# The mixers of a layer in two phases instead of four

## The reference, cut to what matters

```python
h = rmsnorm_2(x, norm1_g) * (1.0 + sc1) + sh1
a, mq, mk, mv, mo, mg, dq, dk, dv = jnp.split(h @ w_in, splits, axis=-1)
conv_l = conv_module(a, ...)      # u = a1 * sigmoid(a2); 31 taps; layernorm over channels; silu
mlstm_l = mlstm_mixer(...)        # 4 heads of 64, forwards and backwards, gates scanned over time
diff_l = diff_mixer(...)          # 4 heads: rotary; p = softmax(q1 k1) - lam * softmax(q2 k2); p @ v; rmsnorm
mix = jnp.concatenate([conv_l, mlstm_l, diff_l], axis=-1)
x = x + g1 * (mix @ w_out)
...
x = x + g2 * peer_ffn(h2, ...)
```

## Time and profile before

| | |
|---|---|
| median of 3 runs | 4462.64 us (4460.4 to 4464.87) |
| the profiled execution's own time | 4458.87 us |
| its span | 4457.1 us |
| TensorE busy | 4037.1 us, 91% |
| DVE, ScalarE, GpSimd busy | 53%, 37%, 34% |
| mean granted TensorE clock | 0.935 |
| layer 0: input blocks / stages 2 to 4 | 945.0 to 1090.7 / to 1336.3 us |
| layer 1: input blocks / stages 2 to 4 | 3224.0 to 3348.5 / to 3511.2 us |

### The profile page before, as it was taken

One profiled execution on the slowest core, in us unless ns is written; L12 is line 12 of the kernel. 1 busy time (PEld: TensorE's weight loads), 2 busy tenths in 40 slices (PEclk: granted clock), 3 DMA queues, 4 the chain that ended last, 5 costly groups with the idle time before them and its releaser, 6 DMA issues. The chain is left out here.

```text
span 4457.1 us, 71091 instructions
## 1 busy us (share of the span) xinstructions
PE 4037.1 (91%) x25218; PEld 3528.5 (79%) x25218; DVE 2383.2 (53%) x4156; ACT 1640.7 (37%) x2529; POOL 1527.5 (34%) x605
## 2 busy tenths in 40 slices
PE   7997698978858999999989999999796699999998
PEld 7974388956525999988879999888684499998887
DVE  4012413144651946687538466885535375667855
ACT  3532204132122443333545433334432245333344
POOL 5840007223002886500028866000060088660000
PEclk9997899989569999999999999999895799999999
DMA  5565545522002554444645544446430155444454
GB/s 185 180 221 178 179 151 152 162 73 80 3 0 90 167 164 138 135 146 146 193 148 164 166 140 136 142 143 190 136 109 12 44 166 174 139 139 141 145 180 151
DMA packets 168398, 613.86 MB, mean 138 GB/s; under 512 B 18592, under 2 KB 20000, under 8 KB 167968
## 3 DMA queue, kind: packets, MB, share of 16 engines
q1 hardware_dynamic: 168224, 611.49, 43.9%
HBM read 610.37 MB, written 1.05 MB: 137 GB/s over the span
## 5 line engine op out<-in xcount | busy, mean ns | idle before, releaser
L1644 POOL TENSOR_TENSOR ring_r<-ring,ring_hi 128x1024 fp32r<-128x1024 f32 x408 | 1065.2, 2618 | 1260.8 <-ACT ring_hi L1781 1259.7
L1781 ACT ACTIVATE ring_hi<-ring 128x1024 fp32r<-128x1024 f32 x792 | 837.8, 1059 | 788.6 <-DMA ring<-in_peer_v 478.4
L1659 PE MATMUL bank<-H_r,ring_hi 128*128 128x256 f32 x3264 | 938.4, 288 | 63.3 <-POOL ring_r L1644 60.3
L1660 PE MATMUL bank<-H_r,ring_hi 128*128 128x256 f32 x3264 | 926.0, 284 | 0.0
L1661 PE MATMUL bank<-H_r,ring_r 128*128 128x256 f32 x3264 | 925.5, 284 | 0.0
L1659 PEld LDWEIGHTS bank<-H_r,ring_hi 128*128 128x128 f32 x3264 | 628.3, 192 | 71.3 <-POOL ring_r L1644 44.9
L277 POOL TENSOR_TENSOR ring_r<-ring,ring_hi 128x1024 fp32r<-128x1024 f32 x183 | 455.3, 2493 | 603.1 <-ACT ring_hi L271 602.6
L1660 PEld LDWEIGHTS bank<-H_r,ring_hi 128*128 128x128 f32 x3264 | 628.6, 193 | 0.0
L1661 PEld LDWEIGHTS bank<-H_r,ring_r 128*128 128x128 f32 x3264 | 628.3, 192 | 0.0
L1711 PE MATMUL bank<-ring_hi,H_r 128*128 128x512 f32 x1536 | 483.8, 396 | 4.5 <-DVE ring_r L1955 4.4
L1713 PE MATMUL bank<-ring_r,H_r 128*128 128x512 f32 x1536 | 474.6, 390 | 0.0
(11 more groups left out here) (312 smaller groups left out, 5469.1 us busy)
## 6 DMA issues: line engine op xcount, KB each, us to landing
ring<-in_peer_u SPq DMA_DIRECT2D x384, 512.0 KB, 3.5
ring<-in_peer_v SPq DMA_DIRECT2D x384, 512.0 KB, 3.5
ring<-in_w_in SPq DMA_DIRECT2D x135, 512.0 KB, 3.5
ring<-in_ada SPq DMA_DIRECT2D x96, 512.0 KB, 5.3
ring<-in_w_f SPq DMA_DIRECT2D x72, 512.0 KB, 3.6
ring<-in_w_br SPq DMA_DIRECT2D x24, 512.0 KB, 3.6
ring<-in_w_q SPq DMA_DIRECT2D x24, 512.0 KB, 3.5
ring<-in_w_out SPq DMA_DIRECT2D x16, 512.0 KB, 3.5
```

The lines of the kernel that those rows point to most:

```text
L1644: pool.tensor_tensor(ring_lo[:, slot, :], ring[:, slot, :], ring_hi[:, m % NH, :].bitcast(F32), ALU.subtract).then_inc(p_lo, 1)
L1659: pe.matmul(o, hi[:, k], x_hi_[:, kt, :], start=(kt == 0), stop=False)
L1660: pe.matmul(o, hi[:, k], x_lo_[:, kt, :], start=False, stop=False)
L1781: act.activation(ring_hi[:, m % NH, :], ring[:, (n0 + m) % NS, :], ACT.Copy).then_inc(a_hi, 1)
```

## The change

Stages 2 to 4 become two things. The scans, the value and state transposes, the rotation and the convolution's norm move into the phase of the input blocks, each behind a certain block; there TensorE now uses banks 0 to 3 for the blocks and waits for the evacuation four before, banks 4 to 7 serve the moved work. The blocks of `w_in` come in another order (gates, convolution, recurrence values, attention values, queries, keys, recurrence keys, queries, output gates). One phase remains: a loop over four heads with four steps each, and an item of the attention in each step (every second step in the last layer). The weights are no longer scaled and subtracted on DVE: DVE writes two diagonal matrices with the factors, and TensorE multiplies each of the two exponentials by its diagonal, which scales, subtracts and transposes at once. The diagonal pieces of the recurrence are masked by a maximum with 10000 in the exponent instead of a product. The convolution's root and the heads' roots come before the reciprocal, with the scale folded in. The large work tile of the recurrence lies where `h_high` was, other tiles in `H`.

```diff
@@ phase of the input blocks @@
+                    pool.memset(Bt, 0.0)
+                    pool.memset(Mx, 0.0)
+                    pool.memset(on, 1.0).then_inc(padded, 1)
+                    for b in range(2):
+                        low(pool, n0, b, a_hi, p_lo)
                     pool.memset(u_pad, 0.0).then_inc(padded, 1)
+                    pool.memset(v_aug, 1.0).then_inc(padded, 1)
...
+                    def turn_values(n, src, b):
+                        pe.wait_ge(by_act, evac[:b + 1].count("act"))
+                        if n:
+                            pe.wait_ge(a_vt, n)
+                        for tt in range(4):
+                            mm = pe.transpose(bank[7][:, tt * P:(tt + 1) * P], src[:, tt * P:(tt + 1) * P], ident)
+                        mm.then_inc(vt_ps, 1)
...
-                        evac_wait(pe, {"act": by_act, "dve": by_dve}, evac, b, 6)
+                        evac_wait(pe, {"act": by_act, "dve": by_dve}, evac, b, 4)
...
+                        if b == 6:
+                            turn_state()
+                        if b in (8, 9):
+                            turn_values(b - 8, mv[:, b - 8, :], b - 3)
+                        if 10 <= b < 14:
+                            turn_values(b - 8, dv[:, b - 10, :], b - 3)
...
+                        if b == 19:
+                            pe.wait_ge(v_tap, 2 * CONV_K)
...
+                        if b >= 17:
+                            rotate(b - 17)
...
                         if b + NH < 25:
                             high(act, n0, b + NH, a_hi)
+                        if b == 0:
+                            act.wait_ge(by_dve, 1)
+                            link(act.activation(Lt, fg, ACT.Abs))
+                            link(act.activation(Lt, Lt, ACT.Exp, scale=-1.0))
+                            act.activation(Lt, Lt, ACT.Ln, bias=1.0).then_inc(a_soft, 1)
...
+                        if 9 <= b < 15:
+                            keep_values(b - 9)
...
@@ the one phase behind it, TensorE @@
+                    def turn_weights(n):
+                        pe.wait_ge(v_p, n + 1)
+                        if n:
+                            pe.wait_ge(a_pt, n)
+                        for k in range(keys_of(n) // P):
+                            o, c = bank[6][:, k * P:(k + 1) * P], slice(k * P, (k + 1) * P)
+                            pe.matmul(o, E[:, n % 2, 0, c], diag[:, n % 2, 0, :], start=True, stop=False)
+                            mm = pe.matmul(o, E[:, n % 2, 1, c], diag[:, n % 2, 1, :], start=False, stop=True)
+                        mm.then_inc(pt_ps, 1)
...
+                        for k in range(4):
+                            if k == 0:
+                                broadcast(h, 0)
+                                products(h, 0)
+                                products(h, 1)
+                                if h:
+                                    values(h - 1, 1)
+                            if k == 1:
+                                broadcast(h, 1)
+                            if k == 2:
+                                products(h, 2)
+                                products(h, 3)
+                            if k == 3:
+                                values(h, 0)
+                            n = item_of(h, k)
+                            if n is not None:
+                                if n + 1 < N:
+                                    scores(n + 1)
+                                if n:
+                                    attend(n - 1)
+                                turn_weights(n)
...
@@ ScalarE @@
+                            if k == 1:
+                                decays(h, 0)
+                            if k == 2:
+                                decays(h, 1)
+                            n = item_of(h, k)
+                            if n is not None:
+                                if n + 1 < N:
+                                    softmax(n + 1)
+                                keep_weights(n)
+                                if n % per_head == 0 and n:
+                                    squares(n // per_head - 1, n)
+                                if n % per_head == 1 and n > per_head:
+                                    root(n // per_head - 1)
...
@@ VectorE @@
+                            if k == 0:
+                                if h:
+                                    finish(h - 1, 0)
+                                exponents(h, 0)
+                            if k == 1:
+                                if h:
+                                    finish(h - 1, 1)
+                                exponents(h, 1)
+                            if k == 2:
+                                weigh(h, 0)
+                                weigh(h, 1)
+                            if k == 3:
+                                weigh(h, 2)
+                                weigh(h, 3)
+                            n = item_of(h, k)
+                            if n is not None:
+                                shares(n)
+                                if n + 1 < N:
+                                    maxima(n + 1)
+                                if n:
+                                    keep(n - 1)
```

More of the change, by code:

```diff
@@ L1244, in build, with item_of @@
             ms = A.take(16)
+            dg = A.take(1)
             tiles = list(range(t0 // P, 4))
+            tall = len(tiles)
+            per_head = 2 if last else 4
+            items = [(h, qt) for h in range(DF_H) for qt in (range(2, 4) if last else range(4))]
+            N = len(items)
+            keys_of = lambda n: T if items[n][1] < 2 else 2 * T
+            def item_of(h, k):
+                if last:
+                    return 2 * h + k // 2 if k % 2 else None
+                return 4 * h + k
@@ new lines, in values @@
+                    def values(h, d):
+                        pe.wait_ge(v_w, 8 * h + 8)
+                        if h or d:
+                            pe.wait_ge(v_h, 2 * h + d)
+                        for tt in tiles:
+                            src = sources(d, tt)
+                            for st in src:
+                                mm = pe.matmul(bank[3][:, tt * 65:tt * 65 + 65], wb[:, d, st, tt * P:(tt + 1) * P],
+                                               v_aug[:, st, h, :], start=(st == src[0]), stop=(st == src[-1]))
+                        mm.then_inc(pv_ps, 1)
@@ new lines, in scores @@
+                    def scores(n):
+                        h, qt = items[n]
+                        for s in range(2):
+                            if n:
+                                pe.wait_ge(a_exp, 2 * (n - 1) + s + 1)
+                            r = slice(64 * s, 64 * s + 64)
+                            pe.matmul(bank[4 + s][:, 0:keys_of(n)], dq[r, h, qt * P:(qt + 1) * P], dk[r, h, 0:keys_of(n)],
+                                      start=True, stop=True).then_inc(ds_ps, 1)
+                    def turn_weights(n):
[7 more added lines that the diff above has]
+                        mm.then_inc(pt_ps, 1)
@@ new lines, in attend @@
+                    def attend(n):
+                        h = items[n][0]
+                        pe.wait_ge(a_pt, n + 1)
+                        if n:
+                            pe.wait_ge(v_o, n)
+                        done = max(0, (n - 1) // per_head)
+                        if n % per_head == 1 and done:
+                            pe.wait_ge(a_root, done)
+                        nk = keys_of(n) // P
+                        for k in range(nk):
+                            mm = pe.matmul(bank[7][:, 0:P], dv_tok[:, k, h * P:(h + 1) * P], pT[:, n % 2, k * P:(k + 1) * P],
+                                           start=(k == 0), stop=(k == nk - 1))
+                        mm.then_inc(o_ps, 1)
@@ L1419, in _ @@
+                    finish(ML_H - 1, 0)
+                    keep(N - 1)
+                    finish(ML_H - 1, 1)
+                    if per_head == 2:
+                        normed(DF_H - 2)
+                    a = tiles[0]
                     hv = hs[:, a:4, :, :].rearrange("p t h e -> p (t h) e")
```

599 lines of the change are left out of this document (269 added, 330 removed).

## The result

The changed kernel takes 4391.1 us (median of 4, 4387.19 to 4394.96) where the kernel before took 4461.52 in the same job (4 runs): ratio 0.9844, 95% interval 0.9827 to 0.9861, some 70 us less. The forecast was 51 us less. Its profiled execution took 4394.96 us, span 4392.9.

A forecast was written before the change was run, and what follows sets the result against it. TensorE, 91% busy, was taken as the bound, with 408.3 us of slow-clock mixer stretches to win from. Gains of 41 us (layer 0) and 10 (layer 1) from 4458.9 gave 4408, 4411 on the median's scale; 8-in-10 range 4365 to 4465.

The forecast's parts named there:

- The sum of layer 0: Layer 0's mixer: blocks 26, before the loop 4, loop 155, tail 19.5, together 204.5 against 245.6 us, gain 41 us.
- Blocks, +26 us each: Input blocks of both layers: moved work and TensorE's waits for ScalarE's copies lengthen each layer's blocks by 26 us.
- rival C: Input blocks: each of ten waits makes 4 us of work run at half rate, 2 us each: 4431 us; chance 0.12.
- Rival D: Input blocks: DVE shuts out GpSimd's low parts, one more stall per layer 4424 us, two more 4436; chance 0.10.
- The new loop of layer 0, 155 us: Layer 0's interleaved loop: 182 us of TensorE work at the lower clock becomes 143, plus 12 us of waits.
- I take half the work at each level: New loop: half of TensorE's work at each clock level, 182 x (0.5 + 0.5 x 0.57) = 143 us in layer 0.
- Preludes and tail: Layer 0 around the new loop: norm phase and preludes go, tails shrink; 4 us before the loop, 19.5 after.
- Layer 1, gain 10: Layer 1's mixer: blocks 26, start 4, loop 108, tail 15, together 153 against 162.7 us, gain 10 us.
- The turn by diagonals: Attention items: eight full diagonal products replace four transposes, 4.0 against 1.12 us; 36 us added TensorE work in layer 0.
- the warm case: Both new phases: if transposes do not count as clock activity, the new turns hold the clock up, as in B.
- A: New phases: clock stays at 1.2 GHz, loops 39 and 25 us longer, 4475 us; chance 0.13.
- B: New phases: clock at 2.4 GHz nearly throughout, 25 us better in each layer, 4361 us; chance 0.15.

The follow-up runs named there:

- two-bank run: The changed kernel with the six value turns alternating between two spare banks, so TensorE waits for the copy one turn later: 4355.25 us, ratio 0.9781.
- combined kernel: The changed kernel with two banks for value turns, backward decays one step earlier, backward value products after their step's scores and read: 4314.36 us, ratio 0.9688.

## Why the prediction was right, and where it was not

The direction and the range held, and the size came near: 51 us were forecast and 70 measured. The account behind it held in part only. The sum of layer 0 (a gain of 41 us, 36 measured) came near by luck, by errors that cancelled; the gain of layer 1 was 23 us more than the sum had; and the loops gained about what I had for layer 0 (16 us forecast, 19 measured), but less by the interleaving than I thought.

**Blocks, +26 us each.** Measured +31.9 and +18. The five waits of 2.2 us were there as forecast, 11 us in all. What failed in layer 0 is that I took the waits to cost no clock, a loss which I had set apart as rival C: each wait also made about 3 us of block work run at the lower clock, and an evacuation comes every 9.98 us against 6.00 without the pause. The two-bank run prices the waits with their clock at 19 us in layer 0. The added work was 10.4 us (151.5 us in that run against 141.1), where the sum had 12.7. In layer 1 I had carried over the kernel before with its stall of 6.3 us. The stall was gone, a gain that the sum did not have; the late low part of block 4 that I put at 2.6 us was a wait of 2.8 (21.3 us in two goes, 18.5 at the start). Rival D, more waits of TensorE for such stalls, did not come. The long low parts did: one took 16.3 us beside the blocks with pauses in layer 0, and nothing waited for it.

**The new loop of layer 0, 155 us.** Measured 152, of which TensorE is busy 126.5 (I had 143) and idle 25.5 (I had 12). The waits were twice mine: the third step's chain is 12.2 us in four waits, about the 12 that I gave it in all, but the value products wait another 7.4 and the turn 5.0 for DVE, which I had not put in. The work was 16 us less. Half the work at each level would be a mean clock of 0.68; it was 0.71, and the key by query products and the scores partly lie in each other's time (a score product starts at 1148.02 us, a key by query product of 1.06 us at 1147.99), which my sum of groups doesn't know. "I take half the work at each level" came near, but for no good reason: in the runs the clock moved with the kind of work (0.57, 0.71 and 0.80 by the turn alone) and with the waits (0.77 and 0.81 when they shrank), and neither is in that phrase.

**Preludes and tail.** 4 us ahead of the loop and 19.5 behind it: measured 6.7 and 18.9. Of the 74.6 us of before 49 went, where the sum had 51. DVE has 99.7 us in the second phase of layer 0; the forecast had 100.

**Layer 1, gain 10.** Measured 33. The blocks gave 8 of the difference, and the loop, forecast at 108 us, took 91: it idles 16.4 us against my 16, and its work is 74.6 against 92. The term mis-sized is the work: the mean clock was 0.76, and again streams overlap. Head and tail took 20.4 where I had 19.

**What the interleaving is worth.** I wrote that it can fill at most 41 us in layer 0. The runs give it 8 to 19 us in both layers together. With it undone, and the diagonals too, some 53 of the 70 us remain: the preludes and tails (58 us in layer 0, less 29 for the longer blocks) and the items, less what the recurrence lost. The items most likely gained by reading an item's values one item later, a reordering that stands in the diff and that my account passed over. I had written that TensorE and DVE take turns in the items; but 34.5 of TensorE's 37.7 idle us there were waits for ScalarE's copy.

**The turn by diagonals.** I charged it with 36 us of added work in layer 0 (by the prediction's own prices 48 less 13.4, which is 34.6). It pays for itself: transposes in its place give the same total, twice the products cost 9 to 15 us, and in the kernel before the products gain 18. The rule that I weighed, that transposes don't count as activity for the clock (the Trainium skill, TensorE: Matmul & The Clock Gate, Part 4), fits the runs: 0.57 with transposes, 0.71 with products, 0.80 with twice as many. It had been set against the forecast as the warm case; the clock did rise with the products, but only part of the way: with the two loops apart the items went at 0.93 and the recurrence at 0.51.

**Rivals.** A, the clock at 1.2 GHz throughout, is out: it was 0.70. B, at 2.4 GHz nearly throughout, is out by the same number. C happened in part: 8.0 us beyond the waits in layer 0 and 3.6 in layer 1, 12 us where its condition gave 20. D is out. Of the signs, TensorE at 80% or more of the loop held (83%), the blocks grew by no more than 35 us (31.9), and the clock lay between 0.7 and 0.8.

## What to carry to other kernels

Read the waits of the busiest engine before crediting an overlap. Here a bank asked for one turn too early cost 28 to 36 us, more than the interleaving of two whole loops was worth; a read issued one item too early stood for 34.5 us of waits in one layer, though no run prices it alone. A short pause of TensorE amid dense work can cost more than its length, since the products behind it may go at the lower clock (19 us for 11 us of pauses in layer 0), so a second bank for a small transposed tile is worth a look even where the pause seems cheap. And replacing DVE scaling and a transpose by products with a diagonal cost nothing in the changed kernel, gained 18 us in the kernel before and some 30 us in the combined one.

Some parts of the change were not tried by themselves: the mask by a maximum instead of a product, the roots ahead of the reciprocals, and each of the pieces that moved beside the blocks.

## What the runs showed of the hardware

A busy TensorE can stand at the lower clock. In the recurrence alone it is busy 71.5 of 75 us at a granted 0.50; its work there is products of 4 and 64 rows and products of 65 columns under full weights. Attention items with transposes go at 0.67 to 0.73, the same items with products of 128 rows and 128 columns at 0.90 to 0.93. Adding such products to a mix raised the mean clock of layer 0's second phase step by step (0.57, 0.71, 0.80) with the time nearly constant (189.9, 180.5, 182.7 us). Which property of the recurrence's products keeps the clock down, rows, columns or the share of weight loads, was not tried.
